# Squared MLP activations 192 instead of 64 bytes past a multiple of 256 in each partition

## The reference, cut to what matters

```python
def sq_relu_mlp(h, w1, w2):
    return jnp.square(jax.nn.relu(h @ w1)) @ w2      # w1: 1024 x 4096, w2: 4096 x 1024
...
x = sublayer_residual(x, sq_relu_mlp(x * (1.0 + sc2) + sh2, mlp_w1[i], mlp_w2[i]), g2, ln_g[i, 1], ln_b[i, 1])
if not last:
    xc = sublayer_residual(xc, sq_relu_mlp(xc * (1.0 + csc2) + csh2, mlp_w1[i], mlp_w2[i]), cg2, ln_g[i, 1], ln_b[i, 1])
```

## Time and profile before

| | |
|---|---|
| median of 3 runs | 1282.27 us (1280.57 to 1283.77) |
| the profiled execution's own time | 1283.15 us |
| its span, first to last instruction | 1281.3 us |
| mean granted clock of TensorE in it | 0.992 |
| PE busy | 1239.1 us, 97% of the span |
| VectorE / ScalarE / GpSimd busy | 888.1 / 572.2 / 97.5 us |
| DMA | 218.44 MB, mean 170 GB/s |

### The profile page before, as it was taken

One profiled execution on the slowest core, in us unless ns is written; L12 is line 12 of the kernel. 1 busy time (PEld: TensorE's weight loads), 2 busy tenths in 40 slices (PEclk: granted clock), 3 DMA queues, 4 the chain that ended last, 5 costly groups with the idle time before them and its releaser, 6 DMA issues.

```text
span 1281.3 us, 23866 instructions
## 1 busy us (share of the span) xinstructions
PE 1239.1 (97%) x10185; PEld 1151.2 (90%) x10185; DVE 888.1 (69%) x1381; ACT 572.2 (45%) x894; POOL 97.5 (8%) x144
## 2 busy tenths in 40 slices
PE   6999999999999999999999999999999888999997
PEld 3899999999988788999998998998999768999997
DVE  4667765677574665587686786786888966767656
ACT  4433347644775454545313213213165655534441
POOL 0111112100001111000010011120100000000000
PEclk8999999999999999999999999999999999999999
DMA  9997898656245463232554456675435103455550
GB/s 345 384 311 240 264 251 204 165 164 195 72 165 174 156 198 132 100 99 87 176 150 137 150 175 197 188 238 161 135 118 198 34 2 132 165 182 182 195 165 34
DMA packets 170283, 218.44 MB, mean 170 GB/s; under 512 B 6224, under 2 KB 147993, under 8 KB 170042
## 3 DMA queue, kind: packets, MB, share of 16 engines
q1 hardware_dynamic: 140328, 148.18, 35.5%
q0 software_dynamic: 29152, 67.42, 17.4%
q10 hardware_dynamic: 698, 1.32, 0.3%
HBM read 215.77 MB, written 1.12 MB: 169 GB/s over the span
## 4 chain that ended last, share of the span: by engine, by line
PE 87%; ACT 4%; DMA 3%; DVE 3%; issue 1%; SPq 1%; POOL 0%; DVEq 0%; ACTq 0%
PE bank L1388 32%; PE bank L723 13%; PE bank L742 10%; PE bank L775 7%; PE bank L758 4%; DMA graw_b<-in_w_mod 2%; PE bank L1293 2%; PE bank L1366 2%; PE bank L833 1%; PE bank L1483 1%; PE bank L1466 1%; PE bank L1545 1%; PE bank L924 1%; DMA pre<-in_w_ada 1%; PE bank L1000 1%
## 5 line engine op out<-in xcount | busy, mean ns | idle before, releaser
L2207 DVE TENSOR_TENSOR wlo<-raw,whi 128x2048 fp32r<-128x2048 f32 x131 | 297.4, 2275 | 88.3 <-ACT whi L1588 87.9
L1588 ACT ACTIVATE whi<-raw 128x2048 fp32r<-128x2048 f32 x131 | 247.9, 1899 | 182.7 <-PE bank L1388 130.4
L1388 PE MATMUL bank<-a_lo,whi 128*128 128x256 f32 (+1 forms) x688 | 165.3, 312 | 0.0
L1388 PE MATMUL bank<-whi,m_hi 128*128 128x256 f32 x576 | 161.0, 279 | 1.2 <-DVE m_lo L2854 0.8
L1388 PE MATMUL bank<-whi,m_lo 128*128 128x256 f32 x576 | 160.3, 278 | 0.0
L1388 PE MATMUL bank<-wlo,m_hi 128*128 128x256 f32 x576 | 160.3, 278 | 0.0
L1388 PEld LDWEIGHTS bank<-a_lo,whi 128*128 128x128 f32 x688 | 112.1, 188 | 8.8
L1388 PEld LDWEIGHTS bank<-whi,m_hi 128*128 128x128 f32 x576 | 108.9, 189 | 1.9 <-DVE m_lo L2854 1.2
L1388 PEld LDWEIGHTS bank<-whi,m_lo 128*128 128x128 f32 x576 | 108.8, 189 | 0.0
L1388 PEld LDWEIGHTS bank<-wlo,m_hi 128*128 128x128 f32 x576 | 108.4, 188 | 0.1
L723 PE MATMUL bank<-h_hi,whi 128*128 128x256 f32 x368 | 104.2, 283 | 0.0
(11 more groups left out here) (459 smaller groups left out, 3200.1 us busy)
## 6 DMA issues: line engine op xcount, KB each, us to landing
raw<-in_mlp_w SPq DMA_DIRECT2D x64, 1024.0 KB, 5.2
raw<-in_w_in SPq DMA_DIRECT2D x32, 1024.0 KB, 7.4
graw_b<-in_w_mod POOLq DMA_DIRECT2D x64, 512.0 KB, 5.1
raw<-in_ev_w_in SPq DMA_DIRECT2D x12, 1024.0 KB, 5.2
pre<-in_w_ada SPq DMA_DIRECT2D x16, 512.0 KB, 9.8
graw_a<-in_w_mod POOLq DMA_DIRECT2D x16, 512.0 KB, 6.7
Y<-in_w_mod POOLq DMA_DIRECT2D x16, 512.0 KB, 4.1
raw<-in_od_w_qkv SPq DMA_DIRECT2D x6, 1024.0 KB, 4.9
```

The source lines that it names most:

```text
L1388: mm = nc.tensor.matmul(o, x, y, start=(k == 0 and i == 0), stop=(k == KT - 1 and i == 2))
L1588: nc.scalar.activation(split_pair(u, kt * cols)[0], landing(u, kt * cols), ACT.Copy).then_inc(hi_done, 1)
L2207: nc.vector.tensor_tensor(split_pair(u, n)[1], landing(u, n), bf(whi[u % HI], n), ALU.subtract).then_inc(lo_done, 1)
```

## The change

Two pads change their size; the second makes up for the first, so that `relu`, `sq` and all that follows keep their places, while `m_hi` and `m_lo` begin 128 bytes lower, at 188608 = 736 x 256 + 192 and 16384 bytes after that. Nothing else is different.

```diff
@@ -255,9 +255,9 @@
             bna = sb("bna", [P, 4, 8], where=e)
             with ExitStack() as e2:
                 cres = sb("cres", [P, 2, D], where=e2)
-                sb("shift_m", [P, 112], where=e2)
+                sb("shift_m", [P, 80], where=e2)
                 m_hi, m_lo = [sb(n, [P, KT, T], f32r, e2) for n in ("m_hi", "m_lo")]
-                sb("shift_relu", [P, 16], where=e2)
+                sb("shift_relu", [P, 48], where=e2)
                 rel_ = sb("relu", [P, T], where=e2)
                 sq_ = sb("sq", [P, T], where=e2)
                 gtmp = sb("gtmp", [P, T], where=e2)
```

## The result

The changed kernel takes 1288.1 us (median of ten runs, 1283.41 to 1289.8), the kernel before 1281.41 us (median of ten, 1279.67 to 1285.2). The ratio is 1.0044, 95% interval 1.003 to 1.0058: slower, by 6.7 us. The profiled execution took 1288.79 us, its span 1287.0 (before: 1283.15 and 1281.3). The forecast had been 1284.1 us with both paces; the range held, and the forecast itself was too low by 4.0 us. It had added +1.8 us to a median of three runs that lay 0.9 us over the median of ten, so the change itself was forecast at +1.8 and measured at +6.7 us.

What follows compares the result with a forecast made beforehand. TensorE was taken to bound the kernel, through matmul time from start to start. Pads and writes at 0 and weight loads at +1.8 us, added to the 1282.27 us median, gave 1284.1 us, range 1277.5 to 1290.5.

Steps and rivals of the forecast that it cites:

- both paces: MLP second projections keep quick (113.3 ns) and slow (117.8 ns) matmuls, reshuffled; 1284.1 us, chance 0.53.
- What bounds the kernel: TensorE, busy 97% of the span: in the MLPs the end moves by matmul time from start to start.
- Pads and writes at nothing: Resized pads and the copies and subtractions writing `m_hi` and `m_lo` cost 0; bounds 3 ns per VectorE instruction.
- The counts and the bounds: Second projections: 962 of 2304 matmuls slow, 1342 quick, 4.45 ns apart; bounds -6.0 and +7.7 us.
- The upper end: Every second-projection matmul slow, +6.0 us, plus the second MLP's first projections, +1.7 us: +7.7 us.
- all slow: All 2304 second-projection matmuls at the slow pace: 1342 quick ones lose 4.45 ns each, +6.0 us.
- What I take: Second projections go from 42% to 60% slow, halfway to 77% in line 723's `h` stretches; +1.8 us.
- Rival 2: Line 1388's weight loads: second projections settle in step with the `w` stream; 1290.4 us at 118.7 ns, chance 0.15.
- Rival 3: Quick pace everywhere in the MLPs' second projections; up to -6.0 us, 1276.3 us, chance 0.12.
- the lower end: All second projections quick, -4.3 us, plus the second MLP's first projections, -1.7 us: -6.0 us.
- Rival 4: Second projections: starts repeat every 128 bytes or play no part; 1282.3 us within a microsecond, chance 0.20.
- What would show it: Chain piece lengths divided by counts on lines 1388 and 1366; pieces ahead of 580 us unchanged, paces 112 to 120 ns.

Runs made afterwards that it cites:

- experiment 5: Against the kernel before: both halves of `a` start 192 instead of 64 bytes beyond a multiple of 256, `m` as before; 1284.51 us, ratio 1.0026.
- experiment 4: Against the kernel before: `m_hi` and `m_lo` both start 128 bytes beyond a multiple of 256; 1290.6 us, ratio 1.0077.
- Experiment 3: Against the kernel before: only `m_lo` starts 192 bytes beyond a multiple of 256, `m_hi` at 64; 1275.01 us, ratio 0.9953.
- experiment 11: Experiment 3 run again, `m_hi` at 64 and `m_lo` at 192, `h` as in the kernel before; 1275.5 us, ratio 0.9962 to that kernel.
- experiment 6: Against the kernel before: high halves of `h`, `a` and `m` at 64, low halves at 192 beyond a multiple of 256; 1278.56 us, ratio 0.9986.
- experiment 7: Against the kernel before: both halves of `m` start on a multiple of 256 (offset 0); 1291.5 us, one run.
- experiment 2: Against the kernel before: only `m_hi` starts 192 bytes beyond a multiple of 256, `m_lo` at 64; 1282.59 us, ratio 1.0015.

## Why the prediction was right or wrong

- **What bounds the kernel: right.** The change of time is found in the distances between matmuls: 6.8 us of it in the MLPs and 0.5 between them, less 1.6 ahead of them, make the 5.7 us between the profiled spans. Neither the clock nor the idle time ahead of the second projections nor another engine moved.
- **Pads and writes at nothing: right.** The median durations of the earlier trace rows stayed within 1 ns, far inside the bound of 3, and the idle time ahead of the second projections is the same to 0.2 us.
- **The counts and the bounds: right.** The prediction had 962 slow of 2304 from the chain; the trace gives 984 of the 2266 that can be counted. The upper end, +6.0 and +1.7 us for all slow, became 5.7 and 1.1.
- **"What I take": wrong, and this is the step that failed.** It said that after the change the difference is that of the stretches in which `h` or `a` moves, "so I expect those paces, in the share in which those stretches have them", and arrived at 60% slow and +1.8 us. The measured share is 99 to 100%, which is 1273 more slow matmuls of the 2266 that can be counted, +5.7 us; with the second MLP's first projections, to which the forecast gave nothing, +6.8. Those stretches are of the other form. In experiment 5 one and the same shift of `a` made it 95% slow as stationary and 11% slow as moving. A pace read with the weights stationary does not carry over to the weights moving, even at the same difference modulo 256.
- **Rival 2, slower: this is what happened, at its "all slow" price.** Its condition, more than 80% slow, was met. Its reason was off: it spoke of settling in step as at 128, and that pace is another one (118.7 ns, experiment 4), which did not come. That the range held is due to this rival: it alone took the upper end to 1290.5, and "slower by over 0.3%", which came, had a chance of 0.28.
- **Rival 3, quick everywhere: did not happen, but the pace was there to be had.** It named the lower end, 1276.3 us. Experiment 3 reaches 1275.0, with the 113.3 ns known from the earlier trace rows and no new pace; it takes the low half alone at 192.
- **Rival 4, no matter: falls.** TensorE: Matmul & The Clock Gate, in the Trainium skill, under "Step-by-step: what each phase is for", which the prediction weighed, has the next weights load through a read port of their own, without taking read bandwidth of SBUF from the running matmul. The runs differ: with nothing changed but the start of the stationary tiles, the same matmul takes 113.3, 117.8, 118.7 or 120.0 ns. The measurement decides; it does not show whether the ports are the reason.
- **What would show it:** most pieces ahead of 580 us kept their lengths (eight of 53 changed by 0.2 us, four each way), and no pace under 112 or over 120 ns came up in the changed kernel.

What is shown: the starts of the stationary halves against the moving weights set which paces occur, and both halves count together. What stays open: by what path the stationary tile's start reaches the matmul's pace, and what chooses between the two paces where a layout has both. The prediction called that choice chance. With 64 / 64 it still looks like it: `h` as moving, in the same layout, is 71% slow in the profile of before and 55% in that of experiment 11.

## What to carry to other kernels

Where PE sets the end and a stream of equal matmuls shows two distances from start to start at full clock, look at where the stationary and the moving tiles start modulo 256, and try pads; here they were worth 1275 to 1291 us with not one instruction changed. Take the share of the paces only from stretches of the same form (the same operand stationary), and be ready for a tile used in both forms to lose in one what it gains in the other, as `a` and `h` did in experiment 6. When a pad moves several tiles that follow each other in one accumulation, move them singly too: the best layout here has one of two tiles where a slower kernel had both.

## What the runs showed of the hardware that was not expected

- A start that differs between the high and the low half (64 and 192) makes the stationary form almost always quick, for three inputs in different stages: 2 to 13% slow, where a common start of 64 gives 31 to 78% for the same inputs. The opposite order (192 and 64) does not: it has a pace of 118.8 to 118.9 ns, with quick stretches between.
- The slowest pace, 120.0 ns, belongs to stationary and moving tiles with the same start (experiment 7), 6.7 ns above the quick one. There the distances are even: 1432 of 1517 in the first MLP are 120 ns.
- A slow pace can be a rhythm: with `m` at 192 and 64 one distance in six is 124 or 125 ns and the rest 117 to 119 (experiment 2), and with both halves at 128 they cycle between 115 and 122 (experiment 4). A share of slow matmuls is then better taken from groups than from single distances.
- Matmuls whose tiles did not move followed their neighbours: the second MLP's first projections went from 366 of 750 slow to 624 of 751 in the changed kernel, to 46 of 747 in experiment 3, and to all 753 in experiment 7.
